# Spacing the parts of the sparse mixer's projection stage: queries and keys taken out of PSUM in three steps, the last key block moved behind the queries, the maxima at one even rate

## The chip, the cores and the metric

The kernel runs on one core of one Trainium2 chip. It is one launch that holds the whole network. The metric is the device time of that launch in microseconds (us), as the median over runs: 3228.9 us for the kernel before (3 runs, 3224.16 to 3230.38 us). The engines go by their names in the profile: PE is TensorE (PEld its weight loads), DVE VectorE, ACT ScalarE, POOL GpSimd, SP SyncE, which issues most loads.

## The reference: what is computed

All tensors are fp32, with 512 tokens of width 1024. Two gated blocks (convolution, neighbourhood and window attention) come first, then a recurrent mixer, a feed-forward block, the sparse mixer, a second feed-forward block and a last norm. The change touches the sparse mixer alone:

```
def nsa_mixer(x, w_in, cmp_pos, cmp_w1, cmp_b1, cmp_w2, w_out):
    proj = x @ w_in                      # 1024 queries, 3 branches of keys and values, 48 gates
    q = q * HEAD_DIM ** -0.5             # 16 heads of 64 in 4 groups, each with its own keys
    k_cmp = compress(kv[0, 0], ...)      # 31 compressed keys: 32 tokens each, two products and a gelu
    v_cmp = compress(kv[0, 1], ...)
    ...
    # branch 0: compressed keys; branch 1: selected blocks; branch 2: the window of 512
    s = q . k - slope * distance;  p = softmax(s, masked);  o_branch = p @ v
    o = gate[0] * o_cmp + gate[1] * o_sel + gate[2] * o_win
    return o @ w_out
```

With 512 tokens there are 8 blocks and 8 are selected, and the window is as long as the sequence, so branches 1 and 2 are causal attention over all keys, each with keys and values of its own.

## The kernel before, in words

**Precision.** A large product is made of three fp32r products. Each operand is split into a rounded part and the rest (`XH`, `XL` for the activations, `WH`, `WL` for the weights), and PE adds high by high, low by high and high by low in one PSUM bank. ACT rounds the weights (L1085), and in this stage POOL makes their rest (L1104).

**The units.** `Plan` writes down the mixer as a list of units (`norder`) before any engine's program exists. Each engine then walks that same list and issues its own part of each unit. An engine works in the order of its queue, so the list sets the order on all of them, and a wait in one unit holds up all that stands behind it on that engine.

**The projection stage** (`nsa_projections`) has 21 turns, one for each block of 128 output columns, in the order of `turns`: blocks 0 to 7 are queries, 12, 13, 16 and 17 keys (`KEYS`), 14, 15, 18 and 19 values (`VALUES`), 8 to 11 feed the compression and 20 holds the gates. A turn has eight steps `("lin", m, k)` of three matmuls (L2705). I write "turn 17 step 6" for index 17 of `turns` and k = 6. Other units are hung at such places with the table `at`:

- `lev` at step 7 takes the finished block out of its bank. For a query block DVE multiplies by the root of the norm (L2985), ACT writes the rounded part of each of two heads (L2896), and DVE the rest of each (L2990). For a key block ACT writes each rounded part twice, to both halves of the partitions (four copies, L2903 and L2904), and DVE writes four rests (L3009). The rests of a key block wait for all four copies, since the second copy of either head has the same key `("nkh2", b, pair)`.
- `rr`, `w1`, `hid`, `c2`, `c2out` are the compression. `hid` is a gelu on ACT, between two loads of an activation table (L2838, L2839).
- `c1`, `cadd`, `cexp`, `ct`, `cpt` are the attention to the compressed keys, once for each tile of 128 queries: scores on PE (L2751), two additions of 128x256 for each half, a maximum and a subtraction on DVE (L3056 to L3066), the exponential on ACT (L2848), a sum, a reciprocal and two products on DVE (L3070 to L3079), and a transpose on PE (L2757).
- `max`, `least`, `sum` are a **maximum**: the softmax of branches 1 and 2 needs the largest score of each row, and the sum, before the scores are made in their transposed form. One of the 128 maxima is two matmuls of 128 to 512 columns (L2765, L2766) to one of three banks of their own, a custom reduction on DVE (L2961), and an exponential with its sum on ACT (L2859), after which the bank is free. PE can so be three maxima ahead of ACT. 32 maxima belong to one group of heads; when they are done, `raise` makes the group's terms (L3086 to L3098), and `far` scales the table of distances for a head (L2953).

**Where the maxima stand** is set by `MOST`. From turn 4 step 4 on each step adds 0.72 of a maximum (0.55 from turn 17 on), and each step of the score stage 1.2.

**Between the stages** stand the units left in `at`, and for each of the four query tiles `q0` (a copy on DVE, L2968, and one on ACT, L2869, into `Q2`) and `rows` (a transpose on PE, L2775, and a copy on ACT, L2874). They put the softmax terms of the first group in place. `rows` uses the banks of the maxima.

**The score stage** (`nsa_scores`) has 80 steps: scores on PE (L2783, L2784, L2788), the exponential on ACT (L2878), the product with the values two or three steps later (L2806), and the other maxima between them.

## Time and profile before

| | us |
|---|---|
| median of 3 runs | 3228.9 |
| the profiled execution | 3228.23 |
| its span | 3226.4 |
| PE busy in the span | 3092.4 (96%) |
| DVE, ACT, POOL busy | 1856.7, 1310.2, 341.7 |
| granted PE clock, mean | 0.989 of full |

A share of busy time is a mean over very different stages. Two other numbers decide how long a stage takes: the time that PE sits idle in it, and the clock that PE was granted. A clock of 1.00 is 2.4 GHz and 0.50 is 1.2 GHz; the mean of a stretch tells how much of it was spent at the lower one. A matmul of 512 columns lists with some 0.39 us, but the next starts 0.23 us after it, so starts are to be compared, not durations.

### The profile page before, as it was taken

The page shows a single profiled execution, that of the slowest core. Times are in us where ns is not written, and L with a number is a line of the kernel's source. Part 1 is how long each engine was busy: PE and PEld are TensorE (multiplying, and loading weights), DVE is VectorE, ACT ScalarE, POOL GpSimd, SP SyncE. Part 2 cuts the span into 40 slices and gives each one's busy share as a digit, 9 for nine tenths or more (in the row PEclk, how much of TensorE's full clock was granted, in tenths as well). Part 3 has the DMA queues.
Part 4 walks back from the last instruction along what each step waited for, and adds up shares of the span by engine and source line. Part 5 has one row for each costly group of instructions (what it writes and reads, how often), then busy time and mean ns, then how long its engine had stood idle before and what let it go on. Part 6 is the DMA issues. An engine that isn't in the chain of part 4 may idle for free.

```text
span 3226.4 us, 37154 instructions
## 1 busy us (share of the span) xinstructions
PE 3092.4 (96%) x14848; PEld 2428.9 (75%) x14848; DVE 1856.7 (58%) x2906; ACT 1310.2 (41%) x2021; POOL 341.7 (11%) x237
## 2 busy tenths in 40 slices
PE   8999999999999999999999999999999889999998
PEld 5877877877788677667667777788887766788887
DVE  5877694454434677673534776666436562466632
ACT  3345534244532344532444474322225556422222
POOL 0011131200000001101220020000003210000000
PEclk9999999999999999999999999999999989999999
DMA  5222142320011422123112233323332310233232
GB/s 208 66 66 73 46 124 79 105 74 27 20 44 57 129 72 82 53 82 106 33 30 63 82 93 92 92 92 98 96 94 75 111 37 1 66 98 92 92 98 72
DMA packets 78733, 251.53 MB, mean 78 GB/s; under 512 B 9120, under 2 KB 11168, under 8 KB 78560
## 3 DMA queue, kind: packets, MB, share of 16 engines
q1 hardware_dynamic: 72672, 227.91, 22.9%
q0 software_dynamic: 5024, 18.09, 1.8%
q10 hardware_dynamic: 864, 3.15, 0.3%
q8 instruction: 118, 1.93, 0.2%
q14 instruction: 55, 0.45, 0.0%
HBM read 247.01 MB, written 2.10 MB: 77 GB/s over the span
## 4 chain that ended last, share of the span: by engine, by line
PE 44%; ACT 4%; DVE 4%; issue 1%; DVEq 0%; ACTq 0%
PE PS L1136 31%; PE PS L1697 3%; PE PS L2705 2%; PE PS L2806 1%; PE PS L1821 1%; PE PS L2783 1%; PE PS L2784 1%; PE PS L2765 1%; ACT WH L1085 0%; PE PS L2727 0%; PE PS L2766 0%; ACT PS L2859 0%; PE PS L2442 0%; ACT L1884 0%; DVE PS L2961 0%
## 5 line engine op out<-in xcount | busy, mean ns | idle before, releaser
L1095 DVE TENSOR_TENSOR WL<-RAW,WH 128x1024 fp32r<-128x1024 f32 (+2 forms) x372 | 432.5, 1163 | 520.4 <-ACT WH L1085 519.7
L1085 ACT ACTIVATE WH<-RAW 128x1024 fp32r<-128x1024 f32 (+4 forms) x425 | 407.6, 965 | 420.4 <-PE PS L1136 322.0
L1697 PE MATMUL PS<-Hh,WH 128*128 128x512 f32 x1376 | 515.6, 375 | 14.3 <-DVE WL L1095 6.5
L1697 PE MATMUL PS<-Hh,WL 128*128 128x512 f32 x1376 | 488.2, 355 | 0.0
L1697 PE MATMUL PS<-Hl,WH 128*128 128x512 f32 x1376 | 488.1, 355 | 0.0
L1697 PEld LDWEIGHTS PS<-Hh,WH 128*128 128x128 f32 x1376 | 260.0, 189 | 76.6 <-issue 23.3
L1136 PE MATMUL PS<-XH,WH 128*128 128x512 f32 x768 | 306.1, 399 | 0.0
L1136 PE MATMUL PS<-XH,WL 128*128 128x512 f32 x768 | 304.4, 396 | 0.0
L1136 PE MATMUL PS<-XL,WH 128*128 128x512 f32 x768 | 304.4, 396 | 0.0
L1697 PEld LDWEIGHTS PS<-Hl,WH 128*128 128x128 f32 x1376 | 260.1, 189 | 44.5 <-issue 7.2
L1697 PEld LDWEIGHTS PS<-Hh,WL 128*128 128x128 f32 x1376 | 261.0, 190 | 38.3
L1552 DVE SCALAR_TENSOR_TENSOR C<-AP,SMA,C 128x512 f32<-128x512 f32 x360 | 242.0, 732 | 0.5
L1104 POOL TENSOR_TENSOR WL<-RAW,WH 128x1024 fp32r<-128x1024 f32 (+1 forms) x67 | 155.8, 2327 | 777.2 <-ACT WH L1085 776.1
L1136 PEld LDWEIGHTS PS<-XL,WH 128*128 128x128 f32 x768 | 144.7, 188 | 36.1 <-issue 1.0
L1136 PEld LDWEIGHTS PS<-XH,WH 128*128 128x128 f32 x768 | 144.6, 188 | 36.0 <-issue 1.0
L1136 PEld LDWEIGHTS PS<-XH,WL 128*128 128x128 f32 x768 | 144.6, 188 | 35.3
L1136 PE MATMUL PS<-FGh,WH 128*128 128x512 f32 x384 | 152.7, 398 | 0.0
L1136 PE MATMUL PS<-FGh,WL 128*128 128x512 f32 x384 | 152.2, 396 | 0.0
L1136 PE MATMUL PS<-FGl,WH 128*128 128x512 f32 x384 | 152.2, 396 | 0.0
L1136 PE MATMUL PS<-Hh,WH 128*128 128x512 f32 (+1 forms) x384 | 140.1, 365 | 5.4 <-DVE Hl L1221 4.3
L1136 PE MATMUL PS<-Hh,WL 128*128 128x512 f32 (+1 forms) x384 | 139.6, 363 | 0.0
L1136 PE MATMUL PS<-Hl,WH 128*128 128x512 f32 (+1 forms) x384 | 139.2, 363 | 0.0
(395 smaller groups left out, 5774.6 us busy)
## 6 DMA issues: line engine op xcount, KB each, us to landing
RAW<-in_w_in SPq DMA_DIRECT2D x124, 512.0 KB, 3.6
RAW<-in_ffn_in SPq DMA_DIRECT2D x96, 512.0 KB, 3.6
RAW<-in_ffn_out SPq DMA_DIRECT2D x48, 512.0 KB, 3.6
RAW<-in_w_ada SPq DMA_DIRECT2D x32, 384.0 KB, 3.6
RAW<-in_nsa_in SPq DMA_DIRECT2D x21, 512.0 KB, 3.3
RAW<-in_lru_in SPq DMA_DIRECT2D x20, 512.0 KB, 3.6
MW<-in_w_ada SPq DMA_DIRECT2D x32, 256.0 KB, 9.7
BS<-in_bs POOLq DMA_DIRECT2D x16, 512.0 KB, 3.9
```

Of the source, the lines that this page charges most:

```text
L1085: act.activation(WH[half[j]][:, 0:n], RAW[j % NRAW][:, 0:n], ACT.Copy).then_inc(*did("act_whi", ("whi", j)))
L1095: dve.tensor_tensor(WL[half[j]][:, 0:n], RAW[j % NRAW][:, 0:n], WH[half[j]][:, 0:n].bitcast(F32), ALU.subtract).then_inc(*did("dve_wlo", ( ...
L1104: pool.tensor_tensor(WL[half[j]][:, 0:n], RAW[j % NRAW][:, 0:n], WH[half[j]][:, 0:n].bitcast(F32), ALU.subtract).then_inc(*did("pool_wlo", ...
L1136: mm = pe.matmul(ps[:, c:c + n], wt[:, 128 * i:128 * i + 128], x[:, a:a + n], start=(seen == 0 and q == 0), stop=(seen == total - 1 and q ...
L1552: dve.scalar_tensor_tensor(dst, src, wt, dst, ALU.mult, ALU.add).then_inc(*did("dve_tap", ("tap", L, m, k, a0), ("tap", L, m, k)))
L1697: mm = pe.matmul(ps[:, c:c + w_], wt[:, 128 * k:128 * k + 128], x[:, a:a + w_], start=(k == 0 and q == 0), stop=(k == n - 1 and q == 2))
L1821: mm = pe.matmul(dst, VV[L, br][:, b, 64 * g:64 * g + 128], src, start=first, stop=end)
L2705: mm = pe.matmul(ps[:, 0:S], wt[half[j]][:, 128 * k:128 * k + 128], x[:, k, :], start=(k == 0 and q == 0), stop=(k == 7 and q == 2))
L2765: pe.matmul(ps[:, 0:n], NQ[:, h, 128 * qt:128 * qt + 128], NKH[b][:, g, 0:n], start=True, stop=False)
L2783: pe.matmul(ps3, NKH[b][:, g, 128 * kt:128 * kt + 128], by_tile(NQ[:, 4 * g:4 * g + 4, :], qt), start=True, stop=False)
L2784: mm = pe.matmul(ps3, NKL[b][:, g, 128 * kt:128 * kt + 128], by_tile(Q2[g % 2], qt), start=False, stop=kt < qt)
L2806: mm = pe.matmul(o[64 * f:64 * f + 64, 0:256].rearrange("p (m q) -> p m q", m=2), VN[b][:, kt, g, :], pt[:, f, :, :], start=(b == 0 and kt ...
```

## The change

Six things are changed, all in the mixer's list of units and what the engines issue for them:

1. Query and key blocks leave their bank in three steps. `lev` keeps only the multiplication on DVE (turn i, step 7). `high` (ACT's copies) comes in turn i + 1 at step 0 for the first head and step 1 for the second, `low` (DVE's rests) at steps 1 and 3. The bank is given up at step 3. A key's rests wait for the copies of their own head only.
2. Key block 17 moves from turn 14 to turn 16, behind the query blocks 6 and 7.
3. `MOST` is 0.65 for all turns from turn 4 step 4 on, except at turn 12 steps 5 and 6 and turn 16 steps 3 and 4 (after the two `hid`), which add nothing; it is 0.8 in the score stage. 82 maxima stand in the projection turns and 7 between the stages (before 89 and 4).
4. The attention to compressed keys of tile qt begins at turn 16 + qt step 6 (before 17 + qt step 2), with its parts at steps 6, 7, 8, 9, 14 and 15 counted from that turn's start.
5. The ACT copy of `q0` (L2869 before) goes to POOL.
6. The four `q0` stand ahead of the other left-over units, and a maximum follows each `rows`.

```diff
-MOST = (0.72, 0.55, 1.2)
+MOST = (0.65, 0.8)
...
         elif u[0] == "lev":
             m = u[1]
-            if m < 8:
-                bank.release(("n", m), ("nq", m))
-            elif m < 12:
+            if 8 <= m < 12:
                 bank.release(("n", m), ("cf", (m - 8) // 2, m % 2))
-            elif m in KEYS:
-                bank.release(("n", m), ("nk",) + KEYS[m])
-            else:
+            elif m in VALUES or m == 20:
                 tmp.take((("n", m), "v"))
                 bank.release(("n", m), (("n", m), "v"))
+        elif u[0] == "low":
+            m = u[1]
+            if u[2] == 1:
+                bank.release(("n", m), ("nq", m) if m < 8 else ("nk",) + KEYS[m])
...
         for qt in range(4):
-            for hf in range(2):
-                at.setdefault((17 + qt, 2 + hf), []).extend([("c1", qt, hf), ("cadd", qt, hf)])
-            at.setdefault((17 + qt, 4), []).append(("cexp", qt))
-            at.setdefault((18 + qt, 1), []).append(("ct", qt))
-            at.setdefault((18 + qt, 2), []).append(("cpt", qt))
-        turns = [0, 1, 12, 16, 20, 2, 3, 8, 9, 4, 10, 11, 5, 13, 17, 6, 7, 14, 15, 18, 19]
+            for step, u in ((6, ("c1", qt, 0)), (7, ("c1", qt, 1)), (7, ("cadd", qt, 0)), (8, ("cadd", qt, 1)), (9, ("cexp", qt)), (14, ("ct", qt)), (15, ("cpt", qt))):
+                at.setdefault((16 + qt + step // 8, step % 8), []).append(u)
+        turns = [0, 1, 12, 16, 20, 2, 3, 8, 9, 4, 10, 11, 5, 13, 6, 7, 17, 14, 15, 18, 19]
         for i, m in enumerate(turns):
...
+            elif m < 8 or m in KEYS:
+                for f in range(2):
+                    at.setdefault((i + 1, f), []).append(("high", m, f))
+                    at.setdefault((i + 1, 1 + 2 * f), []).append(("low", m, f))
...
-                if (i, k) >= (4, 4):
-                    share += MOST[0] if i < 17 else MOST[1]
+                if (i, k) >= (4, 4) and (i, k) not in ((12, 5), (12, 6), (16, 3), (16, 4)):
+                    share += MOST[0]
...
+        for qt in range(4):
+            self.unit("q0", qt)
         for w in sorted(at):
             for u in at[w]:
                 self.unit(*u)
             self.most(1)
         for qt in range(4):
-            self.unit("q0", qt)
             self.unit("rows", 0, qt)
+            self.most(1)
...
+                elif u[0] == "q0":
+                    qt = u[1]
+                    for w in due("pool", ("lin", ("n", 19)), ("qco",), ("pool", "n", turn)):
+                        pool.wait_ge(*w)
+                    turn += 1
+                    pool.tensor_copy(by_tile(Q2[0][64:128, :, :], qt), QCO[64:128, 0:4, qt:qt + 1].broadcast_to([64, 4, 128])).then_inc(*did("pool_q", ("q0c", qt), ("pool", "n", turn)))
...
+        def dve_nsa_low(dve, m, f):
+            src = nbank.of(("n", m))[64 * f:64 * f + 64, 0:S]
+            if m < 8:
+                for w in due("dve", ("nqh", m, f)):
+                    dve.wait_ge(*w)
+                dve.scalar_tensor_tensor(NQ[64:128, 2 * m + f, :], src, 0.125, NQ[0:64, 2 * m + f, :].bitcast(F32), ALU.mult, ALU.subtract).then_inc(*did("dve_st", ("nq", m)))
+            else:
...
+                    for w in due("dve", ("nkh", b, pair, f), ("nkh2", b, pair, f)):
+                        dve.wait_ge(*w)
```

How the order of instructions moves is shown at three places. The rows give line, operation, tiles and size. Line numbers in the changed kernel are up to 9 higher, and an `ISA` pair is one reduction of a maximum and the read of its result.

DVE, around key block 13 leaving its bank, before. `PS` is PSUM, `NKL` the keys' rests:

```order
L2985 TENSOR_TENSOR PS<-PS,RI 128x512
L3009 SCALAR_TENSOR_TENSOR NKL<-PS,NKH 64x512 x4
L2961 ISA PS,NMX<-TBH,PS 128x256
L2961 ISA NMX 128x1
L2961 ISA PS,NMX<-TBH,PS 128x384
L2961 ISA NMX 128x1
```

And in the changed kernel:

```order
L2987 TENSOR_TENSOR PS<-PS,RI 128x512
L2963 ISA PS,NMX<-TBH,PS 128x512
L2963 ISA NMX 128x1
L3012 SCALAR_TENSOR_TENSOR NKL<-PS,NKH 64x512 x2
L2955 TENSOR_SCALAR TBH<-TB 128x512
L2963 ISA PS,NMX<-TBH,PS 128x128
L2963 ISA NMX 128x1
L2963 ISA PS,NMX<-TBH,PS 128x256
L2963 ISA NMX 128x1
L3012 SCALAR_TENSOR_TENSOR NKL<-PS,NKH 64x512 x2
```

The four rests stood together, right behind the multiplication. Now they are two pairs with reductions of maxima ahead of and between them.

DVE, in the attention of the first query tile to the compressed keys, before (`PC` holds its scores, `U` the sums):

```order
L3070 TENSOR_REDUCE U<-PC 128x16
L3073 RECIPROCAL U<-U 128x16
L3076 SCALAR_TENSOR_TENSOR U<-U,RV,GT 128x16
L3079 TENSOR_TENSOR PC<-PC,U 128x512
L2961 ISA PS,NMX<-TBH,PS 128x384
L2961 ISA NMX 128x1
L3002 TENSOR_TENSOR U<-PS,RI 128x512
```

And in the changed kernel:

```order
L3073 TENSOR_REDUCE U<-PC 128x16
L3076 RECIPROCAL U<-U 128x16
L3079 SCALAR_TENSOR_TENSOR U<-U,RV,GT 128x16
L3082 TENSOR_TENSOR PC<-PC,U 128x512
L3012 SCALAR_TENSOR_TENSOR NKL<-PS,NKH 64x512 x2
L2963 ISA PS,NMX<-TBH,PS 128x512
L2963 ISA NMX 128x1
L3012 SCALAR_TENSOR_TENSOR NKL<-PS,NKH 64x512 x2
L3089 TENSOR_TENSOR RUP<-NMX,LSU 128x32
```

The rests of key block 17, and behind them a group's terms, now follow this chain directly.

ACT, from the last turn to the first scores, before (`PTC` is the output of `cpt`, `Q` that of `q0` and `rows`, `PTN` that of the scores' exponential):

```order
L2852 ACTIVATE PTC<-PS 128x512
L2859 ACTIVATE PS,SUM<-PS,NMX 128x256
L2859 ACTIVATE PS,SUM<-PS,NMX 128x384
L2859 ACTIVATE PS,SUM<-PS,NMX 128x512
L2869 ACTIVATE Q<-QCO 64x4x128
L2874 ACTIVATE Q<-PS 4x4x128
L2869 ACTIVATE Q<-QCO 64x4x128
L2874 ACTIVATE Q<-PS 4x4x128
```

And in the changed kernel:

```order
L2861 ACTIVATE PTC<-PS 128x512
L2868 ACTIVATE PS,SUM<-PS,NMX 128x256
L2868 ACTIVATE PS,SUM<-PS,NMX 128x384
L2868 ACTIVATE PS,SUM<-PS,NMX 128x512
L2878 ACTIVATE Q<-PS 4x4x128
L2868 ACTIVATE PS,SUM<-PS,NMX 128x128
L2878 ACTIVATE Q<-PS 4x4x128
L2868 ACTIVATE PS,SUM<-PS,NMX 128x256
```

Between two of the `rows` copies there was a copy from `QCO`, and now the exponential of a maximum.

## Rows read from the trace of the kernel before

**Rows 1.** The page's first line.

```profile
span 3226.4 us, 37154 instructions
```

**Rows 2.** Windows of the mixer: stretch, length, busy by engine, granted clock, DMA.

```profile
2425.00:2535.00 110.00, 105.54 (x525) 85.94 (x524) 74.00 (x181) 62.33 (x151) 30.93 (x16) 1.00 0.28 90
2535.00:2585.00 50.00, 42.72 (x264) 34.82 (x262) 26.33 (x69) 27.45 (x67) 11.86 (x5) 0.90 0.27 93
2585.00:2625.70 40.70, 38.37 (x193) 32.67 (x192) 31.84 (x78) 16.52 (x42) 6.43 (x5) 0.87 0.22 68
2625.70:2636.60 10.90, 7.09 (x31) 4.97 (x32) 7.89 (x24) 6.56 (x18) 4.31 (x3) 0.69 0.04 13
2636.60:2759.10 122.50, 119.59 (x762) 74.31 (x760) 28.30 (x99) 83.00 (x191) 7.66 (x4) 0.99 0.00 1
```

**Rows 3.** Waits in 2425 to 2760: total us, times, longest.

```profile
PE PS L2765 <- ACT PS L2859: 15.1, 16, 3.0
PE PS L2757 <- DVE PC L3079: 4.0, 2, 2.2
```

**Rows 4.** Timeline of 2550 to 2562, around key block 17: start, us, instruction, idle before.

```profile
2550.87 0.70 DVE L2985 TENSOR_TENSOR PS<-PS,RI 128x512 f32<-128x512 f32 x1 [0.78 <-PE PS L2705]
...
2554.08 2.85 DVE L3009 SCALAR_TENSOR_TENSOR NKL<-PS,NKH 64x512 fp32r<-64x512 f32 x4 [2.51 <-ACT NKH L2904]
...
2557.79 0.66 ACT L2859 ACTIVATE PS<-PS,NMX 128x512 f32<-128x512 f32 x1 [2.95 <-DVE NMX L2961]
...
2558.62 0.44 PE L2765 MATMUL PS<-NKH,NQ 128*128 128x384 f32 x1 [2.30 <-ACT PS L2859]
```

**Rows 5.** Window of the matmuls right behind that wait, columns as in Rows 2.

```profile
2559.00:2563.50 4.50, 4.50 (x16) 3.47 (x15) 1.82 (x5) 3.84 (x11) 3.90 (x2) 0.62 0.00 0
```

**Rows 6.** Timeline of 2566 to 2578, the second gelu.

```profile
2570.99 1.28 ACT L2838 ACT_TABLE_LOAD   x1
...
2574.95 0.39 PE L2765 MATMUL PS<-NKH,NQ 128*128 128x256 f32 x1 [2.98 <-ACT PS L2859]
```

**Rows 7.** The chain of waits in 2400 to 2770: start, us, what.

```profile
2429.49 23.20 PE PS L2705 x99
...
2608.80 0.81 PE PS L2751 x8
...
2614.50 0.70 DVE U L3070
...
2615.78 0.69 DVE PC L3079
```

**Rows 8.** Groups by shape in 2425 to 2760: busy us, mean ns, idle before.

```profile
L2961 DVE CUSTOM_DVE_ANT_0 PS<-TBH,PS 128x512 f32<-128x512 f32 x32 | 22.5, 703 | 12.5 <-PE PS L2766 12.2
L2859 ACT ACTIVATE PS<-PS,NMX 128x384 f32<-128x384 f32 x32 | 17.8, 555 | 14.1 <-DVE NMX L2961 14.0
L3059 DVE TENSOR_TENSOR PC<-PC,PS 128x256 f32<-128x256 f32 x8 | 3.4, 421 | 0.3
L2878 ACT ACTIVATE PTN<-PS 128x512 f32<-128x512 f32 x80 | 47.1, 597 | 32.2 <-PE PS L2784 25.5 <-PE PS L2788 5.2
L2859 ACT ACTIVATION_READ_ACCUMULATOR PS<-PS,NMX 128x1 f32 x128 | 25.5, 199 | 0.0
```

**Rows 9.** Timeline of 2619 to 2645, between the stages.

```profile
2629.19 0.69 DVE L3002 TENSOR_TENSOR U<-PS,RI 128x512 f32<-128x512 f32 x1
...
2631.35 1.89 POOL L2673 CAST Q<-QCO 64x2048 fp32r<-64x2048 f32 x1
...
2633.70 1.42 DVE L2968 CAST Q<-NQ 64x512 fp32r<-64x512 f32 x4
...
2635.67 0.59 ACT L2874 ACTIVATE Q<-PS 4x512 fp32r<-4x512 f32 x1
```

**Rows 10.** Timeline of 2513 to 2518, `far` beside a split of POOL.

```profile
2514.01 2.40 POOL L1104 TENSOR_TENSOR WL<-RAW,WH 128x1024 fp32r<-128x1024 f32 x1 [5.61 <-ACT WH L1085]
...
2514.84 1.85 DVE L2953 TENSOR_SCALAR TBH<-TB 128x512 f32<-128x512 f32 x1
```

More of the change, by code:

```diff
@@ L2864, in act_nsa @@
                     act.activation(LSU[:, 32 * g:32 * g + 32], SUM[:, 32 * g:32 * g + 32], ACT.Ln).then_inc(*did("act_ln", ("lsu", g)))
-                elif u[0] == "q0":
-                    qt = u[1]
-                    for w in due("act", ("lin", ("n", 19)), ("qco",)):
-                        act.wait_ge(*w)
-                    act.activation(by_tile(Q2[0][64:128, :, :], qt), QCO[64:128, 0:4, qt:qt + 1].broadcast_to([64, 4, 128]), ACT.Copy).then_inc(*did("act_row", ("q0c", qt)))
                 elif u[0] == "rows":
@@ L2887, in act_nsa, with act_nsa_high @@
                 act.wait_ge(*w)
[L2889 removed]
+        def act_nsa_high(act, m, f):
             nm = ("n", m)
[L2891 removed]
+            src = nbank.of(nm)[64 * f:64 * f + 64, 0:S]
+            for w in due("act", (nm, "scaled"), ("nsa",)):
+                act.wait_ge(*w)
             if m < 8:
[L2893 to L2904 removed]
+                act.activation(NQ[0:64, 2 * m + f, :], src, ACT.Copy, scale=0.125).then_inc(*did("act_st", ("nqh", m, f)))
+            else:
+                b, pair = KEYS[m]
+                dh = NKH[b][:, 2 * pair + f, :]
+                act.activation(dh[0:64, :], src, ACT.Copy).then_inc(*did("act_st", ("nkh", b, pair, f)))
+                act.activation(dh[64:128, :], src, ACT.Copy).then_inc(*did("act_st", ("nkh2", b, pair, f)))
         def act_nsa_gates(act, i):
@@ L2931, in dve_nsa @@
                     dve_nsa_out(dve, u[1])
+                elif u[0] == "low":
+                    dve_nsa_low(dve, u[1], u[2])
                 elif u[0] == "vout":
@@ L2985, in dve_nsa_out @@
                 dve.tensor_tensor(ps[:, 0:S], ps[:, 0:S], RI[:, :], ALU.mult).then_inc(*did("dve_sc", (nm, "scaled")))
-            if m < 8:
-                for f in range(2):
-                    for w in due("dve", ("nqh", m, f)):
-                        dve.wait_ge(*w)
-                    dve.scalar_tensor_tensor(NQ[64:128, 2 * m + f, :], ps[64 * f:64 * f + 64, 0:S], 0.125, NQ[0:64, 2 * m + f, :].bitcast(F32), ALU.mult, ALU.subtract).then_inc(*did("dve_st", ("nq", m)))
             elif m < 12:
```

28 lines of the change are left out of this document (6 added, 22 removed).

## The prediction

> **What bounds the kernel now.** I began with the page's first line for the span, 3226.4 us [rows 1]. The profiled execution took 3228.2 us, 0.7 less than the median of 3228.9. PE is busy 96% of the span, so with the same matmuls only two things make it shorter: less idle time of PE, and less time at the lower clock. Next I read the windows, cut where the mixer changes its work [rows 2]. PE's idle time is length less busy, and the clock's loss is length times one less the granted clock:
>
> - 2425 to 2535 (turns 0 to 12): idle 4.5, clock 0.
> - 2535 to 2585 (turns 13 to 16): idle 7.3, clock 0.10 x 50 = 5.0.
> - 2585 to 2625.7 (turns 17 to 20): idle 2.3, clock 0.13 x 40.7 = 5.3.
> - 2625.7 to 2636.6 (between the stages): idle 3.8, clock 0.31 x 10.9 = 3.4.
> - 2636.6 to 2759.1 (scores): idle 2.9, clock 0.01 x 122.5 = 1.2.
>
> Together 20.8 + 14.9 = 35.7 us is the most that any order of this work can win. The waits name the cause of nearly all the idle time: a maximum waits for the exponential that frees its bank, 16 times, 15.1 us, and the transpose of the compressed scores waits for DVE's product, 4.0 us [rows 3]. So PE does not wait for the projections' own results, but because DVE and ACT fall three maxima behind.
>
> Why they fall behind I read from one case, key block 17 [rows 4]. DVE multiplies at 2550.87, then stands 2.51 us until ACT has made all four copies, then works 2.85 us on the rests. It touches no maximum from 2550.87 to 2556.93, 6.1 us. ACT gets its next reduced maximum at 2557.79 after idling 2.95 us, and PE stood 2.30 us. Behind that wait the mean clock is 0.62 over 4.5 us [rows 5], so PE went from 2.4 to 1.2 GHz and came back: 0.38 x 4.5 = 1.7 us more. I count 1.7 us for each wait of about 2 us. The second gelu is the other pattern: ACT loads a table at 2570.99, and PE's maximum at 2574.95 stood 2.98 us [rows 6].
>
> **The change part by part.** Prices used: a step of the projections is 3 x 0.234 = 0.70 us of PE [rows 7]; a maximum has 320 columns in the mean, so 0.29 us of PE (2 x 0.234 x 320 / 512; I use 0.3), a reduction 0.70 x 320 / 512 = 0.45 us of DVE, and on ACT 0.50 and the read 0.20 [rows 8].
>
> *Three steps for queries and keys.* No instruction is added; they move. DVE no longer waits 2.51 us for four copies, and its four rests of 0.71 us come in pairs with reductions between them. For key block 13, DVE's work in the next turn is the multiplication 0.7, the rests 2.85, five reductions 2.3 and `far` 0.4: 6.3 us. PE's turn is 8 steps 5.6 and five maxima 1.5, over 7.1 us with a `w1` on top. DVE keeps up, and the three banks cover the order within the turn. The waits of blocks 13 and 17 in this stretch go, with their clock.
>
> *No maxima behind `hid`.* ACT is away from 2570.99 to about 2574.2 (0.75 of an exponential ahead of 2574.95): 3.2 us. With steps 3 and 4 of turn 16 left out, PE needs a bank that ACT frees after the gelu only at step 7, five steps and two maxima or 4.1 us later, with a `c1` of 0.8 [rows 7] on top. The wait of 2.98 us goes, with its clock.
>
> So for 2535 to 2585 I take idle 7.3 to 1.0 and clock 5.0 to 0: **-11.3 us**. Bounds: -12.3 (nothing left), -5 (two of the waits stay with their clock, each some 2 + 1.7).
>
> *Turns 0 to 12.* The rate falls from 0.72 to 0.65 and the query and key blocks there are spread. The blocks for the compression (four products in one piece) and the `rr` additions stay as they are, and part of the idle time is theirs. 4.5 to 2.0: **-2.5 us** (bounds -4, 0).
>
> *Turns 17 to 20.* Here the change loads more on DVE. Block 17's rests now stand in turn 17, where a query tile's chain is too, and the rate rises from 0.55 to 0.65. From the end of block 17 to the reduction of maximum 64 DVE has in its order: the multiplication 0.7; eight instructions of 256 columns (four additions, four copies of `c2out`) 8 x 0.42 = 3.4 [rows 8]; maximum and subtraction 1.4; the sum to the last product 2.0 (2614.50 to 2616.47 [rows 7]); the rests 2.85; a group's terms 1.2 (five instructions of 32 columns, each less than the 0.42 of 256); `far` 0.4; four reductions 1.8: 13.8 us. The exponential that frees the bank adds 0.5. PE, up to maximum 67 that takes this bank, has nine steps 6.3, six maxima 1.8, three `c1` 2.4 and one `ct` 0.4: 10.9 us. So PE is 3.4 us short of work, in two or three waits, the largest over 2 us. From then on DVE has 9.0 us a turn (0.7, 1.7, 1.4, 2.0, `vout` 0.7, 5.2 x 0.45, 0.2) against PE's 9.6 (5.6, 1.6, 0.4, 0.4, 1.6) and catches up slowly. I take idle 3.4 and twice 1.7 of clock, 6.8 against 7.6 now: **-0.8 us**. Bounds: -6 (the banks hide it), +12 (each of four turns waits 2 us and runs a third of itself at 1.2 GHz).
>
> *Between the stages.* Now DVE is late: the last block ends at 2625.7 and its multiplication stands at 2629.19 [rows 9]. In the new order the last chain is done two thirds of a turn earlier, and by the sums above DVE is 1.1 us late. Then on DVE the multiplication 0.7, a reduction 0.5, the four casts of `q0` 1.4 [rows 9], a reduction of 512 columns 0.7; on ACT its exponential 0.85, then copy 0.59, exponential 0.5, copy 0.59, exponential 0.65, copy 0.59, exponential 0.75; and PE's last short maximum 0.2: 9.1 us from block 19 to the first score. POOL's four copies of `q0` are each a quarter of the one at 2631.35 by size, 0.47 us (bounds 0.47 and 1.89). ACT needs the first after 5 us and one each 1.2 us, so they are hidden, and cost 2.8 us at the upper bound. But behind them POOL goes straight to the two large casts for the next group, 2 x 1.89 us, and DVE's casts now fall beside these, which they did not before: 2633.70 is after 2633.24. `far` at 2514.84 took 1.85 us in place of some 0.42, and ended 0.28 after the POOL instruction that began before it [rows 10]. So a DVE cast can wait out a POOL cast, once or twice: bounds 0 and 3.8, and I take 1.5. 10.6 against 10.9 now; the stretch also holds three maxima more (0.9) and one transpose less (0.4), taken out of the turns: 10.6 - 10.9 - 0.5 = **-0.8 us** (bounds -3, +4).
> The Trainium skill ("SBUF — State Buffer", "SBUF: two separate sides") calls the second port of DVE an exclusive lock shared with POOL, held for the whole instruction. By it the casts would wait out both large ones, 3.8 us in place of 1.5, and the sum would be 2.3 us higher. The trace agrees on the kind of wait, in the `far` of 1.85 us; no run so far shows it for these casts.
>
> *Scores.* ACT's step holds 0.60 + 1.2 x 0.7 + 0.2 x 0.59 = 1.56 us [rows 8, 9] against PE's 122.5 / 80 = 1.53: it is the bound while the maxima last. With 0.8 it is 1.28, and PE's waits go. Idle 2.9 to 0.7, clock 1.2 to 0: **-3.4 us** (bounds -4.1, -1). The last group's terms now come at score step 48, four steps or 6 us ahead of their first use, against 1.2 us of DVE for them.
>
> Sum: -11.3 - 2.5 - 0.8 - 0.8 - 3.4 = -18.8 us. 3228.2 - 18.8 = 3209.4, and with the 0.7 to the median **3210 us**.
>
> **The rivals.**
>
> 1. *The waits move to turns 17 to 20.* DVE is at 9.0 of 9.6 us a turn there, and a split of POOL can stretch an instruction of it by over 1 us. If each turn waits 2 us and pays 1.7 of clock, that is 14.8 in place of 6.8, 8 us back, and 2 more between the stages: 3220 us. For it: the sum above, and `far` at 1.85. Against: DVE had 31.8 of 40.7 us there, and PE idled only 2.3 [rows 2].
> 2. *It does nothing much.* DVE and ACT are short in total, and a new order only shifts who waits: within 6.5 us of now, about 3226 us. Against: in 2425 to 2535 ACT is busy 62.3 of 110 us and DVE 74.0 [rows 2].
> 3. *Slower.* In turns 17 to 20 the waits follow each other so closely that PE stays at 1.2 GHz. Its work there is 38.4 - 5.3 = 33 us at full clock and 66 at half: +25, less the 17.2 won in the first two stretches and the scores: +8, 3237 us. It decides from a wait of about 2 us in every half turn on. Now the mean clock there is 0.87 [rows 2].
>
> **How the numbers follow.** Forecast 0.62 (3203 to 3217), rival 1 0.20, rival 2 0.11, rival 3 0.05, still faster than 3203 0.02. The range to the far side of rival 1, 3202 to 3224, leaves some 0.18 outside. About 0.2%, 6.5 us, is what a measurement of this kernel can tell from no change. Faster by more 0.84 (forecast, rival 1, still faster), the same 0.11, slower 0.05.
>
> **What would show it.** Right: in the changed profile no wait of a maximum over 1 us in turns 13 to 16 and clock 1.00 there; DVE's rests with hardly any idle time before them; the waits of maxima gathered in turns 17 and 18; some 10 to 11 us from block 19 to the first score; PE idle under 1 us in the scores. Wrong: a mean clock below 0.85 in turns 17 to 20, or waits over 2 us in each of them (rival 1 or 3); a total of waits of maxima still near 15 us (rival 2); or a first score later than 12 us after block 19.

## The result, and the profile after

The changed kernel took 3208.8 us (median of four runs, 3204.57 to 3209.48) against 3228.0 us before. The ratio is 0.9942, with a 95% interval of 0.9930 to 0.9953: 19.2 us less, where I had forecast 3210 and a range of 3202 to 3224. The profiled execution took 3208.35 us. The page's first lines; behind them stand busy time, share of the span and instructions of each engine:

```profile
span 3206.5 us, 37159 instructions
PE 3081.9 (96%) x14848; PEld 2423.6 (76%) x14848; DVE 1861.1 (58%) x2906; ACT 1307.9 (41%) x2017; POOL 344.0 (11%) x241
```

Against [rows 1] the span is 19.9 us shorter, with the same 14848 matmuls. To see where, I cut both traces at the same places of the program: the first matmul of turns 0, 13 and 17, the end of block 19, the first and the last matmul of the scores. The cuts of [rows 2] were round times; with these both kernels hold the same blocks in each stretch. Columns: stretch, its length, busy time of PE, PEld, DVE, ACT and POOL with instructions, granted clock, DMA share, GB/s. First the kernel before:

```profile
2424.55:2527.57 103.02, 98.96 (x480) 80.31 (x479) 69.39 (x170) 56.80 (x139) 30.93 (x16) 1.00 0.30 96
2527.57:2579.75 52.18, 44.57 (x279) 36.45 (x278) 27.22 (x74) 31.11 (x74) 11.86 (x5) 0.90 0.27 91
2579.75:2625.49 45.74, 43.34 (x221) 36.87 (x219) 35.79 (x85) 18.18 (x46) 6.43 (x5) 0.89 0.20 61
2625.49:2636.66 11.17, 7.36 (x33) 5.00 (x33) 8.10 (x24) 6.83 (x18) 4.31 (x3) 0.69 0.04 12
2636.66:2759.00 122.34, 119.43 (x761) 74.20 (x758) 28.30 (x99) 82.94 (x191) 7.66 (x4) 0.99 0.00 1
```

And the changed one:

```profile
2425.12:2521.27 96.15, 95.50 (x469) 78.86 (x468) 65.58 (x157) 53.03 (x126) 30.95 (x16) 1.00 0.30 102
2521.27:2561.48 40.21, 39.85 (x290) 34.04 (x289) 23.94 (x62) 28.63 (x67) 11.97 (x5) 1.00 0.32 118
2561.48:2605.68 44.20, 39.51 (x214) 33.06 (x212) 41.17 (x101) 20.95 (x53) 6.90 (x6) 0.96 0.15 52
2605.68:2619.66 13.98, 8.63 (x36) 5.39 (x35) 11.08 (x25) 7.21 (x21) 6.30 (x6) 0.76 0.15 47
2619.66:2738.10 118.44, 118.30 (x769) 75.30 (x768) 31.30 (x110) 84.15 (x198) 7.57 (x4) 1.00 0.00 1
```

Read the first and second column against each other. In turns 13 to 16 PE's idle time fell from 7.6 to 0.4 us and the clock from a loss of 5.2 to none. In the scores the idle time fell from 2.9 to 0.1. Between the stages it rose from 3.8 to 5.35. By stretch the change is -6.9, -12.0, -1.5, +2.8 and -3.9 us. That is -21.5; the mixer also begins 0.6 us later, and what follows the scores takes 1.0 us more. The stretches don't hold quite the same work in both kernels: turns 0 to 12 have 42 maxima in place of 48 and turns 13 to 16 have 20 in place of 23, but also the first query tile's two `c1`, which stood in turn 17 before; the scores have 39 maxima in place of 35.

PE's waits in 2420 to 2760 (total us, times, longest):

```profile
PE PS L2774 <- ACT PS L2868: 8.2, 4, 3.8
PE PS L2766 <- DVE PC L3082: 1.3, 1, 1.3
PE PS L2724 <- DVE U L2999: 0.7, 1, 0.7
```

Sixteen waits of a maximum, 15.1 us [rows 3], are now four of 8.2 us, and two of these four, 3.26 and 3.76 us, are nearly all of it. The rests of a key block, which before began after 2.51 us of idle time [rows 4], now stand like this for key block 13 (start, us, instruction, idle before):

```profile
2531.80 0.70 DVE L2987 TENSOR_TENSOR PS<-PS,RI 128x512 f32<-128x512 f32 x1
...
2533.77 1.40 DVE L3012 SCALAR_TENSOR_TENSOR NKL<-PS,NKH 64x512 fp32r<-64x512 f32 x2 [0.62 <-ACT NKH L2904]
...
2537.12 1.42 DVE L3012 SCALAR_TENSOR_TENSOR NKL<-PS,NKH 64x512 fp32r<-64x512 f32 x2
```

The first of the two waits that are left is in turn 17, where block 17 and the first query tile's chain now meet:

```profile
2560.55 0.70 DVE L2987 TENSOR_TENSOR PS<-PS,RI 128x512 f32<-128x512 f32 x1 [3.16 <-PE PS L2714]
...
2566.32 0.55 DVE L2963 CUSTOM_DVE_ANT_0 PS<-TBH,PS 128x384 f32<-128x384 f32 x1
...
2569.05 1.39 DVE L3012 SCALAR_TENSOR_TENSOR NKL<-PS,NKH 64x512 fp32r<-64x512 f32 x2
```

ACT in the same stretch, and PE:

```profile
2566.43 0.63 ACT L2857 ACTIVATE PC<-PC 128x512 f32<-128x512 f32 x1 [3.32 <-DVE PC L3069]
2567.09 0.59 ACT L2903 ACTIVATE NKH<-PS 64x512 fp32r<-64x512 f32 x1
2567.71 0.59 ACT L2904 ACTIVATE NKH<-PS 64x512 fp32r<-64x512 f32 x1
2568.32 1.06 ACT L1088 ACTIVATE WH<-RAW 128x1024 fp32r<-128x1024 f32 x1
2569.40 0.56 ACT L2868 ACTIVATE PS<-PS,NMX 128x384 f32<-128x384 f32 x1
...
2570.13 0.43 PE L2774 MATMUL PS<-NKH,NQ 128*128 128x256 f32 x1 [3.26 <-ACT PS L2868]
```

DVE reduced this maximum of 384 columns at 2566.32, yet the exponential that frees its bank begins only at 2569.40. ACT had stood 3.32 us until DVE had subtracted the maximum of the compressed scores (L3069), and then its queue held 2.9 us of other work: their exponential, the two copies of block 17's second head, and a rounding of weights. So PE waits for ACT's queue, which a late DVE had held up.

The second is between the stages. Compare this with [rows 9]: the four casts of DVE took 1.42 us there, beside no work of POOL.

```profile
2608.17 5.04 DVE L2970 CAST Q<-NQ 64x512 fp32r<-64x512 f32 x4
...
2608.67 1.89 POOL L2678 CAST Q<-NQ 64x2048 fp32r<-64x2048 f32 x1
...
2610.63 1.97 POOL L2682 CAST Q<-QCO 64x2048 fp32r<-64x2048 f32 x1
...
2613.90 0.66 ACT L2868 ACTIVATE PS<-PS,NMX 128x512 f32<-128x512 f32 x1 [4.89 <-DVE NMX L2963]
```

PE's row behind it in the same trace:

```profile
2614.73 0.58 PE L2774 MATMUL PS<-NKH,NQ 128*128 128x256 f32 x1 [3.76 <-ACT PS L2868]
```

DVE is in its casts from 2608.17 to 2613.21, POOL in its two from 2608.67 to 2612.60. Behind the casts stands a reduction, behind it the exponential at 2613.90, and behind that PE at 2614.73. So one collision explains this wait by the order of the trace; that it is the cause is what the first experiment asks. POOL's four small copies of `q0` took 0.61 us each, not the 0.47 of the forecast, and were hidden as it had said.

### The profile page after: what moved, and what is told of

Same layout as the page of the kernel before. It is cut to its first block, busy times and chain, and to the rows that moved or that the text cites. A ratio compares the mean times of both kernels' runs of the same rounds, so it can differ in the third digit from the quotient of the medians.

```text
span 3206.5 us, 37159 instructions
## 1 busy us (share of the span) xinstructions
PE 3081.9 (96%) x14848; PEld 2423.6 (76%) x14848; DVE 1861.1 (58%) x2906; ACT 1307.9 (41%) x2017; POOL 344.0 (11%) x241
## 4 chain that ended last, share of the span: by engine, by line
PE 45%; DVE 3%; ACT 3%; issue 1%; DVEq 0%; ACTq 0%
PE PS L1139 31%; PE PS L1700 3%; PE PS L2714 3%; PE PS L2815 1%; PE PS L1824 1%; PE PS L2792 1%; PE PS L2793 1%; PE PS L2774 0%; PE PS L2775 0%; PE PS L2736 0%; ACT WH L1088 0%; PE PS L2445 0%; ACT L1887 0%; DVE PS L2963 0%; PE PS L2784 0%
```

## The experiments

Eleven more kernels, and the changed one a second time, ran in three comparisons, each with the kernel before beside it. The lengths of the five stretches in us, cut as above, and the time (median of all runs of that kernel). The kernel before had a median of 3225.8 us in the comparison of e1, e2, e3 and e5, 3227.9 in that of e4, e6, e7 and e8, and 3227.7 in that of e9 to e11 and of the changed kernel again. Medians of different comparisons can so be off by 2 us against each other, and the ratio is the better measure:

```
kernel             0-12   13-16  17-20  between  scores | median   ratio to before [95%]
before            103.0   52.2   45.7   11.2    122.3   | 3228.0
changed            96.2   40.2   44.2   14.0    118.4   | 3208.8   0.9942 [0.9930, 0.9953]
changed, again     96.2   40.3   47.1   13.9    118.5   | 3208.4   0.9940 [0.9927, 0.9953]
e1_pool_later      96.2   40.6   47.0    9.8    118.4   | 3204.6   0.9938 [0.9924, 0.9951]
e2_no_spacing      97.8   42.0   49.8   14.0    118.4   | 3217.1   0.9970 [0.9958, 0.9981]
e3_rates_alone     98.1   44.6   42.3   14.5    120.2   | 3212.7   0.9956 [0.9944, 0.9968]
e4_no_gap          99.7   41.6   46.7    9.0    118.5   | 3211.1   0.9952 [0.9940, 0.9965]
e5_chain_late      96.2   38.6   45.2   18.0    119.2   | 3213.6   0.9958 [0.9945, 0.9970]
e6_own_head       102.6   50.7   42.2   10.8    122.4   | 3222.9   0.9989 [0.9980, 0.9998]
e7_scores_08      103.1   52.2   43.8   11.5    118.2   | 3224.5   0.9990 [0.9981, 0.9999]
e8_gap_17          96.2   40.6   45.0    9.9    121.9   | 3209.7   0.9944 [0.9931, 0.9956]
e9_no_move         96.2   38.9   41.2   15.3    119.1   | 3206.8   0.9933 [0.9921, 0.9946]
e10_copies_on_act  96.2   40.4   45.3   10.4    118.7   | 3205.0   0.9926 [0.9913, 0.9938]
e11_small_gap      96.2   40.2   47.7    9.4    119.8   | 3208.3   0.9938 [0.9924, 0.9951]
```

The stretches are of one profiled execution each. Turns 17 to 20 change from run to run by 3 us in the same program (changed, and changed again; where they differ is told below), and by 1.9 us between before and e7, which are the same program up to the scores; the others change by a few tenths. The -1.5 us of the changed kernel's first profile in these turns is therefore not shown to be a gain: its second has +1.3.

**POOL's large casts later.** The two casts for the next group wait until the last copy of the first group's rows is made.

```
-free = [("lin", ("n", 19))] if g == 1 else ...
+free = [("lin", ("n", 19)), ("nrow", 0, 3)] if g == 1 else ...
```

> The changed kernel, with POOL's two large casts of the next group held back until the last of the first group's rows copies is done. Theory (POOL's casts block DVE's four casts of q0, which took 5.04 us beside them against 1.42 us alone in the trace before): the four casts take about 1.4 us again, the wait of 3.76 us of PE behind them becomes about 0.5, and the first score comes 3 to 3.5 us earlier: 3205 to 3206 us where the changed kernel has 3208.8. Rival (the casts were long for another reason, such as POOL's four small copies just ahead, or ACT is the bound there anyway): casts still 4 to 5 us, or a first score less than 1 us earlier, and the time unchanged.

DVE's casts and the stretch:

```profile
2613.41 1.67 DVE L2970 CAST Q<-NQ 64x512 fp32r<-64x512 f32 x4
```

```profile
2610.93:2620.68 9.75, 6.29 (x35) 3.56 (x35) 7.57 (x25) 7.20 (x21) 2.45 (x4) 1.00 0.23 67
```

5.04 us became 1.67, and the stretch lost 4.2 us. PE's wait behind it fell to 1.70 us, not to the 0.5 expected. Of the 4.2 us, 3.4 are the casts themselves, and 0.9 is PE: from the end of its wait to the first score it took 4.93 us in the changed kernel, where it was partly at the lower clock, and 4.07 here. The three later kernels with the same hold-back (e8, e10, e11) have 9.4 to 10.4 us there, and those in which POOL's two large casts came among DVE's four right behind block 19 (changed, changed again, e2) 13.9 to 14.0. That the collision cost about 4 us is shown. The whole time cannot show it: the runs were 3204.6 three times and 3209.1 and 3210.0, and the interval overlaps that of the changed kernel.

**The changed kernel without the spacing.** All four copies and rests come right behind the multiplication, as before; what a rest waits for (its own head's copy) stays new.

```
-  at (i+1, f): ("high", m, f);  at (i+1, 1+2f): ("low", m, f)
+  behind ("lev", m): ("high", m, 0), ("high", m, 1), ("low", m, 0), ("low", m, 1)
```

> The changed kernel, with ACT's copies and DVE's rests of a query or key block issued again at step 7 of its own turn, right behind the multiplication (the rests still wait for their own head's copies only). Theory (the spacing is what removed the waits of maxima behind query and key blocks): turns 0 to 12 lose 2 to 4 us, blocks 13 and 6, 7 in turns 13 to 16 bring back one or two waits of 1 to 2 us with 1.7 us of clock each: 3214 to 3218 us. Rival (the lower rate and the gaps behind the gelus did it, and the spacing is worth little): within 2 us of 3208.8.

Turns 13 to 16 and 17 to 20:

```profile
2523.75:2565.75 42.00, 40.74 (x289) 33.81 (x288) 23.54 (x61) 28.25 (x65) 11.96 (x5) 1.00 0.34 113
2565.75:2615.59 49.84, 42.83 (x214) 35.04 (x212) 43.63 (x101) 21.23 (x55) 6.92 (x6) 0.90 0.14 46
```

PE's wait for maxima is nine times, 12.8 us, in place of four times, 8.2. The kernel lost 8 to 9 us of the 19: 1.7 and 1.8 us in the first two stretches, and in turns 17 to 20 5.6 us against the first profile of the changed kernel, 2.8 against the second. PE's idle time there is 7.0 us, against 4.7 and 3.4. So by these single profiles the spacing is worth most where I had not looked for it: where DVE is short of time, not in turns 13 to 16. The spacing alone, on the kernel before, was not run.

**The rates alone, on the kernel before.** The rates, the two gaps and a maximum behind each `rows`; nothing of the spacing, the move or the casts.

```
-MOST = (0.72, 0.55, 1.2)
+MOST = (0.65, 0.8)     # and no maximum at (12,5) (12,6) (16,3) (16,4); most(1) after each rows
```

> The kernel before, with nothing but the new rates: 0.65 of a maximum a step, none at the two steps behind each gelu, a maximum behind each rows, and 0.8 in the score stage. Theory (several parts each carry their own share): the scores win 3 to 4 us, the gap behind the second gelu 4 to 5, the waits behind key blocks 13 and 17 stay: 3228 less 8 to 10, so 3218 to 3220 us. Rival (the rates are all of it): 3209 to 3212 us. Second rival (without the spacing the rates bring only the scores' share): 3224 us.

```profile
2424.22:2522.27 98.05, 96.53 (x468) 78.56 (x467) 65.27 (x157) 52.66 (x126) 30.90 (x16) 1.00 0.31 100
2522.27:2566.87 44.60, 41.20 (x273) 32.93 (x272) 26.21 (x63) 28.82 (x65) 11.91 (x5) 0.96 0.30 99
2566.87:2609.18 42.31, 39.87 (x226) 33.10 (x224) 36.86 (x96) 20.75 (x55) 6.43 (x5) 1.00 0.24 74
```

3212.7 us: against its own kernel before, the rates win 13 us by medians and 14 by the ratio, of 19, where I had expected 8 to 10. By `e7` below the rate of the score stage alone gives 3 to 4. What the rest of the change adds, 5 us, is not settled by the whole time: the two intervals overlap. Turns 13 to 16 went from 52.2 to 44.6, with key block 17 still in them and its rests still waiting for all four copies: DVE stood 10.1 us before the rests of the key blocks, as before (10.0), but the waits of maxima of 1.86 and 2.30 us behind blocks 13 and 17 were 1.52 and 0.89. I take it that with fewer maxima to work off at the same time the same stall of DVE costs less. Which of the rate and the gap did it in these turns, this run doesn't separate.

**The gaps taken out of the changed kernel.**

```
-if (i, k) >= (4, 4) and (i, k) not in ((12, 5), (12, 6), (16, 3), (16, 4)):
+if (i, k) >= (4, 4):
```

> The changed kernel, without the two gaps: turn 12 steps 5 and 6 and turn 16 steps 3 and 4 add maxima like all others. Theory (ACT is away 3.2 us for a gelu with its two table loads, and the gap is what keeps PE off a bank that ACT has yet to free): a wait of 1 to 3 us comes back in turn 16, with 1.7 us of clock, and 0.5 to 1 us in turn 12, and turns 13 to 16 take 43 to 45 us in place of 40.2: 3211 to 3214 us. Rival (the rate of 0.65 alone leaves enough room): no wait over 0.5 us there, and the time within 1.5 us of the changed kernel.

```profile
2524.57 0.50 PE L2774 MATMUL PS<-NKH,NQ 128*128 128x512 f32 x1 [2.40 <-ACT PS L2868]
```

3211.1 us, by medians some 2 us worse, within the two intervals. The wait came at the first gelu, at the end of turn 12, and not at the second, where I had expected it: turn 16 had none, though the clock of turns 13 to 16 was 0.96. With the new rate the maxima fall on other steps, so which gelu needs a gap may be a matter of phase. Turns 0 to 12 became 3.5 us longer (two maxima more are 0.6 of it), turns 13 to 16 1.4, and the wait in turn 17 grew from 3.26 to 4.42 us.

That the whole lost so little has another cause: the stretch between the stages took 9.0 us in place of 14.0, though POOL's casts were not held back.

```profile
2614.27 2.66 DVE L2970 CAST Q<-NQ 64x512 fp32r<-64x512 f32 x4
...
2616.79 1.89 POOL L2678 CAST Q<-NQ 64x2048 fp32r<-64x2048 f32 x1
```

DVE's four casts stood beside POOL's small copies of `q0` (2613.69 to 2616.65), the last one began at 2616.1, and only then came POOL's first large cast. In the changed kernel DVE reached its casts 2.5 us behind the end of block 19, here 0.9. So with nearly the same list of units the collision comes or stays away by less than 2 us, and this run says little about what the gaps alone are worth.

**The compressed chain four steps later.** In the changed kernel, `c1` to `cpt` at steps 10, 11, 11, 12, 13, 18 and 19 in place of 6, 7, 7, 8, 9, 14 and 15.

> The changed kernel, with the attention to the compressed keys begun four steps later, at turn 17 + qt step 2 as before the change. Theory (in turn 17 DVE has block 17's rests and a tile's chain at once, and that is the wait of 3.26 us with its clock): the wait in turn 17 shrinks to under 1.5 us, but the last chain ends four steps later, so that DVE is late at the end of block 19 and the stretch between the stages grows by 2 to 4 us: 3207 to 3211 us in all. Rival (the order in turn 17 does not matter, the sum of DVE's work over turns 17 to 20 does): the wait only moves, turns 17 to 20 stay at 44 us, and the end grows: 3211 to 3213 us.

3213.6 us. The rival was the nearer: the wait only moved, to 2.66 us early in turn 18, turns 17 to 20 took 45.2 us, and the tail grew by 4.0 us to 18.0. DVE's last chain ran into it and its casts still took 4.58 us beside POOL. With block 17 in turn 17 the early chain is worth some 5 us by the ratios; the two intervals overlap between 0.9945 and 0.9953.

**A rest waits for its own head's copy, on the kernel before.**

```
-("nkh2", b, pair)      +("nkh2", b, pair, f)      # at the copy, and where the rest waits
```

> The kernel before, with one key split in two: a key block's rests wait for ACT's copies of their own head only, not for all four. Theory (half of what the key blocks cost is the 2.51 us for which DVE stands idle): DVE's idle time before the rests falls from 2.5 to some 1.2 us a block, the waits of maxima behind blocks 13 and 17 shorten by about 1.2 us each, and 1 to 4 us are won: 3222 to 3225 us where before has 3226. Rival (the rests themselves hold up the maxima as long): under 1 us won.

```profile
DVE NKL L3009 <- ACT NKH L2904: 5.1, 4, 1.3
```

DVE's idle time before rests of keys halved, from 10.0 us, and block 17's wait fell from 2.30 to 1.06 us; PE's waits for maxima stayed at 15.8 us. Eleven runs: 3222.9 against 3227.9, ratio 0.9989 [0.9980, 0.9998], so between 0.6 and 6.5 us less. In its profile turns 13 to 16, where the edit works on blocks 13 and 17, are 1.5 us shorter. The 3.5 us in turns 17 to 20, which hold no key block, are nearly all clock (1.00 against 0.89), and I put them down to what varies from run to run there.

**The scores' rate alone, on the kernel before** (1.2 to 0.8 in the third entry of `MOST`).

> The kernel before, with 0.8 of a maximum a step in the score stage in place of 1.2, and nothing else. Theory (ACT is the bound of the score stage while it has 1.2 maxima a step, 1.56 us against PE's 1.53): PE's idle time of 2.9 us in that stage falls under 1 us and the clock stays up, and the stage gets 3 to 4 us shorter: 3222 to 3223 us where before has 3226. Rival (the stage's waits have another cause, such as the copies into NKL for the next group): idle still over 2 us, time unchanged.

```profile
2638.05:2756.20 118.15, 118.01 (x760) 74.88 (x758) 28.71 (x99) 82.82 (x190) 7.57 (x4) 0.99 0.00 1
```

PE's idle time in the scores fell from 2.9 to 0.14 us and the stretch by 4.2, all that the change won there. The rate was not enough in e3, whose scores took 120.2 us: there PE was never idle for long either (0.6 us), but the mean clock was 0.98, since the stage began at 1.2 GHz behind a stretch at 0.66. The whole time is 0.9990 [0.9981, 0.9999].

**A gap in turn 17.** With the casts later (as in the first experiment), no maxima in steps 1 to 6 of turn 17, and 0.9 in the scores to work off those left.

> The changed kernel with POOL's large casts held back as in e1_pool_later, and a third gap: turn 17 steps 1 to 6 add no maximum, and the score stage takes 0.9 a step (43 maxima there in place of 39). Theory (the wait of 3.26 us in turn 17 and the low clock behind it come from maxima that queue behind DVE's 13.8 us of other work): no wait of a maximum over 1 us in turns 17 to 20 and clock 1.00 there; turns 17 to 20 take 39 to 41 us in place of 44 to 47, the scores 1 us more: 3198 to 3202 us. Rival (the wait turns into one of the compressed scores' transpose for DVE's product, which is late for the same reason): turns 17 to 20 at 43 us or more, 3203 to 3206 us.

```profile
2568.82 0.81 PE L2766 MATMUL PS<-CO,PC 128*128 128x128 f32 x4 [2.28 <-DVE PC L3082]
```

The maximum's wait in turn 17 went and the transpose of the compressed scores waited 2.28 us in its place; a maximum waited 1.61 us at 2604.01; and at 0.9 the scores took 121.9 us. DVE is late in turn 17 whoever waits for it. 3209.7 us, no gain, and worse than theory and rival had said.

**The changed kernel again.** One program, to see how turn 17 varies.

> The changed kernel once more, unaltered. In its first profile the wait of 3.26 us in turn 17 was followed by 1.8 us of lost clock; in that of e1_pool_later, whose program is the same up to there, the same 3.26 us were followed by some 6 us. Theory (the length of the low clock behind one and the same wait differs from run to run, which is where the two groups of times near 3204.6 and 3209 us come from): the profile shows a wait of 3.2 to 3.3 us there and a clock loss of either 1.7 or about 5 us behind it, turns 17 to 20 take 44 or 47 to 49 us, and the runs again fall at 3204 to 3205 and 3208 to 3210 us. Rival (the difference belongs to the two kernels): again 44.2 us and 1.8.

```profile
2564.46:2611.52 47.06, 43.71 (x214) 36.89 (x212) 41.24 (x101) 20.97 (x53) 7.15 (x6) 0.85 0.15 48
```

The same wait of 3.26 us stood at 2573.12. The clock behind it did not go the same way. The first profile of the changed kernel, from that wait on:

```profile
2570.10:2584.00 13.90, 12.69 (x63) 10.64 (x63) 13.16 (x31) 5.33 (x14) 4.65 (x3) 0.88 0.18 58
```

And the second:

```profile
2573.10:2587.00 13.90, 13.88 (x47) 11.95 (x48) 11.23 (x29) 5.33 (x14) 3.59 (x3) 0.53 0.18 58
```

A clock of 0.88 over 13.9 us is 1.7 us lost, one of 0.53 is 6.5. In the second PE was at 1.2 GHz for nearly all of this stretch, and was never idle in it, and DVE, busy for 11.23 of the 13.90 us in place of 13.16, had caught up. Turns 17 to 20 took 2.9 us more and the whole execution 4.7 (3213.05 against 3208.35; 2.9 us of it lie ahead of the mixer, and later parts give 1.1 back). The first experiment's profile had 0.54 there. I could not choose which of the two a run gets. Nor is this shown to be what spreads the whole times: the five runs were 3203.8, 3208.0, 3208.4, 3210.8 and 3213.1 us, not two groups as I had expected, and more than half of the 4.7 us between the two profiles lies ahead of the mixer.

**The four copies of `c2out(1)` on ACT**, with the casts later.

```
-dve.tensor_copy(VB[32*q:..., :, 64*q:...], p1[...])          # x4
+act.activation(VB[32*q:..., :, 64*q:...], p1[...], ACT.Copy) # x4
```

> The changed kernel with POOL's large casts held back as in e1_pool_later, and c2out's four copies of turn 17 (4 x 0.42 us) made by ACT instead of DVE. Theory (what holds PE in turn 17 is the sum of DVE's work): the wait of 3.26 us shrinks by about 1.7 us to some 1.5 us, the clock behind it stays up or loses one step of 1.7, turns 17 to 20 take 41 to 42.5 us and the whole 3199 to 3203 us. Rival (ACT, which then has 1.7 us more ahead of its exponentials, holds the banks instead): the wait stays over 2.5 us and the time at 3205 to 3210 us.

```profile
2568.70 0.39 PE L2774 MATMUL PS<-NKH,NQ 128*128 128x256 f32 x1 [1.47 <-ACT PS L2874]
```

```profile
2561.84:2607.18 45.34, 41.39 (x214) 34.23 (x212) 39.66 (x97) 21.81 (x55) 6.92 (x6) 0.92 0.16 50
```

```profile
2565.00 0.63 ACT L2863 ACTIVATE PC<-PC 128x512 f32<-128x512 f32 x1 [0.85 <-DVE PC L3070]
```

Four copies of 0.42 us less on DVE, and PE's wait in turn 17 fell from 3.26 to 1.47 us. The path is the one seen above: DVE's subtraction comes sooner, ACT stands 0.85 us for it in place of 3.32, and its exponential begins 4.1 us behind block 17's multiplication in place of 5.9; the rest of ACT's queue is as it was. So DVE's load sets the length of that wait, though PE waits for ACT. That the copies now stand on ACT itself did no harm: ACT had been idle. The forecast for the stage failed all the same: turns 17 to 20 took 45.3 us, not 41 to 42.5, with waits of 1.06 and 1.32 us behind the first and a clock of 0.92, and the time, 3205.0 us, lies at the rival's edge. All five runs lie in 3201.8 to 3205.5, with a ratio of 0.9926 [0.9913, 0.9938], the lowest ratio of all. Beside the changed kernel in the same comparison (3208.4, 0.9940 [0.9927, 0.9953]) the intervals overlap: better by 3 us in the median, and not settled.

**The same with a small gap**, steps 1 to 3 of turn 17, and 0.84 in the scores.

> As e10_copies_on_act, and turn 17 steps 1 to 3 add no maximum, with 0.84 of one a step in the score stage. Theory (with DVE's load lower, the three steps take away what is left of the wait): no wait over 1 us in turns 17 to 20, clock 1.00, turns 17 to 20 at 40 to 41 us, the scores at 119 to 120, the whole 3198 to 3202 us. Rival (as in e8_gap_17, the transpose of the compressed scores then waits for DVE's product, and the added rate costs in the scores): no better than e10_copies_on_act.

3208.3 us. A wait of 2.55 us came at 2580.07, in turn 18, and the clock over turns 17 to 20 was 0.86: the load was put off, not removed, as the rival had said.

**Block 17 back at its old turn, the chain late, in the changed kernel** (chain from step 4 of each turn, as before).

```
-turns = [..., 5, 13, 6, 7, 17, 14, 15, 18, 19]
+turns = [..., 5, 13, 17, 6, 7, 14, 15, 18, 19]
```

> The changed kernel with key block 17 back at turn 14, ahead of the query blocks 6 and 7. The attention to the compressed keys must then begin later, at turn 17 + qt step 4 (block 7's rests come at step 3 of turn 17). Theory (the move and the early start belong together: they trade DVE's late finish for a crowded turn 17): turn 17 has no wait over 1.5 us, but the last chains run on behind block 19, the stretch between the stages takes 17 to 20 us in place of 14, and the whole is 3209 to 3214 us. Rival (the move was needed for the maxima in turns 13 to 16 too): turns 13 to 16 also lose 2 us or more, 3214 to 3217 us.

```profile
2562.59:2603.76 41.17, 39.43 (x226) 33.24 (x225) 34.58 (x94) 19.70 (x55) 6.33 (x5) 1.00 0.21 67
2603.76:2619.07 15.31, 9.69 (x41) 6.08 (x41) 11.69 (x33) 8.00 (x23) 6.74 (x7) 0.67 0.09 33
```

3206.8 us, 0.9933 [0.9921, 0.9946], less than theory and rival had said: the move with its early chain brought nothing that can be measured. Turns 13 to 16 are as clean as with it (38.9 us; the first tile's two `c1`, some 1.6 us, stand in turn 17 here), turns 17 to 20 have clock 1.00 and take 41.2 us, and the tail pays 15.3 us, with a wait of 3.98 for a DVE that is late with the last block. DVE's casts took 1.42 us here, since POOL's large ones began after them.

## Why the prediction was right, and where it was not

The time was right, 3210 against 3208.8, and most of the mechanism; two terms were off by about 3 us each, in opposite directions.

*Turns 13 to 16, -11.3.* Measured -12.0. No maximum waited there, the clock was 1.00, and DVE stood 0.62 us and then not at all before block 13's rests. Over all key blocks it stood 3.2 us in place of 10.0, so "hardly any" was a little too much. But which edit did it I had put too simply: I gave it all to the spacing and the gap. By e3 the rates and gaps alone win 7.6 of the 12 us; by e2 the spacing adds 1.8 when all else is there; by e4 the gaps add 1.4. My reading is that the stall of DVE and the density of maxima had to meet for PE to wait.

*Turns 0 to 12, -2.5.* Mis-sized. The stretch is 6.9 us shorter. 3.4 of it is idle time (4.1 to 0.65): six waits of 0.23 to 1.00 us became one of 0.51. The other 3.5 is busy time. PE has 11 matmuls fewer here, two to a maximum, so six maxima have gone to later stretches, at 0.3 each 1.8 us. That is work moved and not saved, and the sum rightly left it out. Like for like the term is 5.1 us against 2.5: 0.9 too little for the idle time, and 1.7 of busy time that I had put at nothing and can't name.

*Turns 17 to 20, -0.8.* DVE's sum for turn 17 held: 13.8 us from block 17's multiplication to the end of the reduction of maximum 64 (2560.55 to 2574.37). PE was to be 3.4 us short and waited 3.26 us, and e10 shows that DVE's load sets the length. The place was another: I had maximum 67 wait for the bank of 64, but it was maximum 65 that waited for the exponential of 62, behind 2.9 us of ACT's own work, for which the sum had nothing. No run takes ACT's part away by itself. Idle plus clock was 4.7 + 1.8 = 6.5 us against my 6.8. But the second profile has 3.4 + 7.1 = 10.4 with the same wait. The step that failed is "I count 1.7 us for each wait of about 2 us": it was read off one window [rows 5], and it is one of at least two outcomes. That the first profile agrees with 6.8 to a few tenths is luck. So a loss of clock far above 1.7 us does occur from turn 17 on, but rival 1 as a whole did not: there was neither a wait over 2 us in every turn nor a mean clock below 0.85. The sign that I had given, waits gathered in turns 17 and 18, held for one of the four waits; the 3.76 us stood between the stages.

*Between the stages, -0.8.* Wrong in size: 10.6 us forecast, 14.0 measured, beyond the 12 us that I had named as the sign of an error. I saw that POOL's casts would fall beside DVE's and took 1.5 us, nearer to `far` [rows 10] than to the bound of 3.8. The four casts took 5.04 in place of 1.42, +3.6: DVE waited out both of POOL's casts, nearly the upper bound. That is 2.1 of the 3.4 us that are missing. Another 0.9 is PE, slower behind its wait than in e1, for which I had nothing, and 0.4 I can't name. e1 took the collision away and got 9.75 us. The trace agrees with the Trainium skill ("SBUF — State Buffer", "SBUF: two separate sides") that whichever of the two engines begins later is blocked for the other's whole instruction: two of DVE's four casts lasted 2.10 and 2.11 us beside POOL's of 1.89 and 1.97. The 3.8 us that I derived from it was the right price here; in e4, where DVE's casts came first, there was hardly any. `far` was the wrong row to lean on: it met the last part of one instruction, whereas these casts were queued against two.

*Scores, -3.4.* Measured -3.9, with four maxima more in the stage, and -4.2 by e7, with the rate alone.

Sum: -18.8 against -19.2 by medians and -19.9 by profiles. In idle time and clock, the two things that I had counted, the five stretches fell by 19.4 us. But I gave turns 0 to 12 2.6 us too little gain and the stretch between the stages some 3 us too little cost, turns 17 to 20 differ by 3 us from one run to the next, and the 1.6 us by which the mixer began later and the rest of the network took longer I had put at nothing: the agreement to 1 us is partly luck.

What stays open: what the spacing alone, or the rate without the gaps, would do to the kernel before; what the collision and the gaps are worth apart in e4; why the clock after one and the same wait loses 1.7 us in one run and 6.5 in another; 1.7 us of busy time in turns 0 to 12; and whether 3205.0 is truly below 3208.4.

## What to carry to other kernels

When PE waits for a bank, look first at how fast work is handed to the slower engines, and only then at the order inside one block: here the rates with two gaps were worth 13 to 14 of 19 us (3 to 4 of them, by e7, from the score stage), and undoing the spacing cost 8 to 9. When a move makes a POOL instruction that reads SBUF fall beside short DVE copies, price it at POOL's whole instruction, for each one in POOL's queue, and ask which of the two comes first: the stretch took 14.0 us where POOL's casts came among DVE's, and 9.0 in e4, where DVE had begun its last one before them. When a sum of one engine's work gives the wait, go through the queue of the engine behind it too: in turn 17 the exponential stood behind 2.9 us of ACT's own work. Price a wait of PE at its length plus a range of clock, from several profiles of one kernel, not from one window.
